# RWKV-7 layer inside a two-layer trunk: output projection tiles moved into the last head pair's products, its queries computed in quarters

## The reference

```python
def wkv7_scan(S0, r, w, k, v, a, b):
    def step(S, inp):
        r_t, w_t, k_t, v_t, a_t, b_t = inp
        sa = jnp.einsum('bhvk,bhk->bhv', S, a_t)
        S = S * w_t[:, :, None, :] + sa[..., None] * b_t[:, :, None, :] + v_t[..., None] * k_t[:, :, None, :]
        return S, jnp.einsum('bhvk,bhk->bhv', S, r_t)
...
    r = heads(xr @ w_rkv[0])
    k = heads(xk @ w_rkv[1])
    v = heads(xv @ w_rkv[2])
...
        y = (y + bonus).reshape(B, L, D_MODEL).astype(dtype)
        return (y * g) @ w_out
```

## Time and profile before

| | us |
|---|---|
| median of 3 runs | 2353.7 (2351.63 to 2355.56) |
| the profiled execution | 2355.08 |
| its span, first to last instruction | 2353.2 |
| TensorE busy | 2275.5 |
| VectorE busy | 1569.6 |
| ScalarE busy | 1267.3 |
| the last pair, from its scores (L1422) to its variance (L1607) | 1261.6 to 1318.0 |

### The profile page before, as it was taken

How to read it: one execution, slowest core, us unless ns; L and a number is a source line. 1 busy time by engine, 2 the same in 40 slices (tenths; PEclk the granted TensorE clock), 3 DMA queues, 4 the chain that set the end, 5 groups by cost and what they waited for, 6 DMA issues and landing times.

```text
span 2353.2 us, 57929 instructions
## 1 busy us (share of the span) xinstructions
PE 2275.5 (97%) x25142; PEld 1872.2 (80%) x25142; DVE 1569.6 (67%) x1784; ACT 1267.3 (54%) x1399; POOL 201.4 (9%) x200
## 2 busy tenths in 40 slices
PE   8999999999999899999998899999999999999998
PEld 4677666888888478888887688888888888888886
DVE  2544685322233676666665288888888888888888
ACT  4422024322232555555554277878787778787774
POOL 2000561100000040000001020000000000000010
PEclk9999999999999999999999999999999999999999
DMA  8556216233232521211102489999999999999994
GB/s 279 196 215 232 91 45 207 72 107 89 90 105 92 166 68 56 62 59 59 56 25 70 182 326 366 375 370 371 386 357 377 364 382 361 378 368 380 360 391 170
DMA packets 228493, 512.00 MB, mean 218 GB/s; under 512 B 15271, under 2 KB 108223, under 8 KB 228031
## 3 DMA queue, kind: packets, MB, share of 16 engines
q1 hardware_dynamic: 225470, 498.61, 58.5%
q10 hardware_dynamic: 1730, 7.10, 0.9%
q0 software_dynamic: 1152, 4.19, 0.6%
HBM read 492.58 MB, written 17.30 MB: 217 GB/s over the span
## 4 chain that ended last, share of the span: by engine, by line
PE 89%; DVE 4%; ACT 3%; DMA 2%; issue 1%; POOL 0%; ACTq 0%; SPq 0%; DVEq 0%
PE bank L1719 27%; PE bank L1749 13%; PE bank L1202 4%; PE bank L1203 3%; PE bank L1204 3%; PE bank L1108 2%; PE bank L1079 2%; PE bank L1080 2%; PE bank L1081 2%; PE bank L1327 2%; PE bank L1363 2%; PE bank L1220 2%; PE bank L1219 2%; PE bank L1221 2%; PE bank L1374 2%
## 5 line engine op out<-in xcount | busy, mean ns | idle before, releaser
L3121 DVE TENSOR_TENSOR w_low<-expert_w,w_high 128x1792 fp32r<-128x1792 f32 (+2 forms) x384 | 771.8, 2024 | 120.8 <-ACT w_high L2283 118.1
L2283 ACT CAST w_high<-expert_w 128x1792 fp32r<-128x1792 f32 (+2 forms) x384 | 652.0, 1701 | 217.0 <-PE bank L1719 144.5
L1719 PE MATMUL bank<-w_high,xg_high 128*128 128x448 f32 x1024 | 294.2, 368 | 4.0 <-DVE xg_low L3111 4.0
L1719 PE MATMUL bank<-w_high,xg_low 128*128 128x448 f32 x1024 | 293.1, 367 | 0.0
L1719 PE MATMUL bank<-w_low,xg_high 128*128 128x448 f32 x1024 | 293.1, 367 | 0.0
L1719 PEld LDWEIGHTS bank<-w_high,xg_high 128*128 128x128 f32 x1024 | 191.6, 189 | 21.3 <-DVE xg_low L3111 4.1
L1719 PEld LDWEIGHTS bank<-w_high,xg_low 128*128 128x128 f32 x1024 | 192.8, 188 | 16.9
L1719 PEld LDWEIGHTS bank<-w_low,xg_high 128*128 128x128 f32 x1024 | 192.9, 188 | 15.8
L1749 PE MATMUL bank<-w_high,hid_high 128*128 128x512 f32 x448 | 175.8, 392 | 0.0
L1749 PE MATMUL bank<-w_high,hid_low 128*128 128x512 f32 x448 | 174.9, 390 | 0.0
L1749 PE MATMUL bank<-w_low,hid_high 128*128 128x512 f32 x448 | 174.7, 390 | 0.0
(11 more groups left out here) (442 smaller groups left out, 4063.8 us busy)
## 6 DMA issues: line engine op xcount, KB each, us to landing
expert_w<-in_moe_w_dram SPq DMA_DIRECT2D x128, 1792.0 KB, 9.7
expert_w<-in_moe_w_dram SPq DMA_DIRECT2D x32, 2048.0 KB, 10.6
arena<-in_mod_w_dram SPq DMA_DIRECT2D x48, 1024.0 KB, 8.3
expert_w<-in_moe_w_dram SPq DMA_DIRECT2D x32, 1536.0 KB, 10.3
arena<-in_ffn_w_dram SPq DMA_DIRECT2D x44, 512.0 KB, 5.1
slot_rows<-arena SPq DMA_DIRECT2D x25, 512.0 KB, 5.5
arena<-in_hy_w_in_dram SPq DMA_DIRECT2D x12, 1024.0 KB, 5.3
arena<-in_rw_w_rkv_dram SPq DMA_DIRECT2D x48, 256.0 KB, 2.9
```

Of the source, the lines that this page charges most:

```text
L1719: last = pe.matmul(bank[b0 + v][:, 0:EH], x[:, k, :], w_[:, kk, v * EH:v * EH + EH], start=(k == 0 and x is XGH and w_ is wh), stop=(k == ...
L2283: act.copy(high_piece(kind, n), piece(kind, ering[q % ERN], n // 2, n % 2))\
L3121: dve.tensor_tensor(piece(kind, low[s], n // 2, n % 2), piece(kind, ering[s], n // 2, n % 2), high_piece(kind, n).bitcast(F32), ALU.subtract)\
```

## The change

Three things are edited. `OUT_LIST` gives the projection tiles a new order: first the 16 tiles of k = 0 to 3 whose sums lie in banks 2 and 3, then the 16 of the same k in banks 6 and 7, then the rest as before. Fourteen tiles are issued inside m, n and the out products of the last pair, two at a time at seven places, and so fourteen fewer after the variance. And the queries of the last pair (`ahead_queries(7, ...)`, issued at the end of pair 6) are computed in four slices of 64 columns where there were two of 128; this makes 16 more products of the source, which are 64 instructions more ahead of the last pair's level loop.

```diff
         OUT_ORDER = (0, 2, 4, 6, 1, 3, 5, 7)
+        OUT_LIST = [(k, m) for ms in (OUT_ORDER[0:2] + OUT_ORDER[4:6], OUT_ORDER[2:4] + OUT_ORDER[6:8]) for k in range(4) for m in ms]
+        OUT_LIST += [(k, m) for k in range(4, KT - 1) for m in OUT_ORDER]
...
+                width = C if j == KT - 1 else P
                 for k in tiles:
-                    for t in range(SEQ // P):
-                        cs = slice(t * P, t * P + P)
+                    for t in range(SEQ // width):
+                        cs = slice(t * width, t * width + width)
...
-                for t in range(first, last):
-                    k, m = t // KT, OUT_ORDER[t % KT]
-                    if t % KT == 0:
+                for k, m in OUT_LIST[first:last]:
+                    if m == 0:
                         pe.wait_ge(sem("ld_out"), 16 * (k + 1))
...
                     d, b = divmod(x, NB)
+                    if x == NB and not more:
+                        out_products(0, 2)
...
+                    if not more and x % 2 == 0:
+                        out_products(2 + x, 4 + x)
...
                 for d in range(2):
+                    if not more:
+                        out_products(10 + 2 * d, 12 + 2 * d)
...
-                    out_products(0, 2)
+                    out_products(14, 16)
...
-                        out_products(2 * st, 2 * st + 2)
+                        out_products(14 + 2 * st, 16 + 2 * st)
...
-                    out_products(16, 19)
+                    out_products(30, 33)
...
-                    out_products(19, 23)
+                    out_products(33, 37)
...
-                    out_products(23, OUT_TILES)
+                    out_products(37, OUT_TILES)
```

## The result

The changed kernel takes 2358.5 us (median of 20 runs), the one before 2353.1: a ratio of 1.0028, 95% interval 1.0020 to 1.0035. It is slower by 0.28%. The profiled execution has a span of 2357.8 us against 2353.2; the changed kernel's profile is 2.6 us ahead where the last pair's queries begin (1252.88 against 1255.49), in code that is the same in both, so the last pair loses more than the two spans differ by. The time lies in the predicted range, but a clear loss had been given 2 chances in 10.

The account below looks back on a forecast made before the run. TensorE, busy nearly all of the span, was taken as the bound, with stops awaiting blocks of its program. Queries 3.6, first round 1.7, switching 1.8 and stops -5.0 gave +2.1 us: median 2355.8, range over the cases 2350.5 to 2359.5.

Parts of the forecast that it names:

- Queries: Last pair's query products: 64 of 64 columns, each costing what one of 128 does, +3.6 us (bounds 0 and +3.6).
- Ahead of the loop: Before the last pair's level loop: a block boundary falls just ahead of it; no cost was put in the sum.
- First round: Level loop's first round: two inner boundaries stop TensorE, the second for 2.0 us; +1.7 us taken, between 0 and +3.7.
- Behind the loop: L1402, after the level loop: its 0.43 us stop goes, since the boundary moves inside the loop and the block is there.
- m, n and out: Last pair's m, n and out products: moved tiles cover the 2.95 and 1.66 us stops; seven insertions cost +1.8 us.
- the tail: Projection tiles after the variance: fourteen fewer take off 6.05 us, and the same 6.05 us come in m, n and out.
- switching: Seven insertions of tiles among 64x64 products, 0.26 us each for changing tile shapes: +1.8 us, bounds 0 and 7 x 0.35.
- A rule against the trace: Skill's rule that block crossings are mostly hidden: moved tiles cover nothing, so the sum would be 3.6 + 1.8 = +5.4 us.
- The rival of a block missed behind the loads: A boundary in wu (L1507) gets its block one weight transfer later: price +2.9, total +5.0 us, 2358.7; chance 0.17.

Follow-up runs that it names:

- e2: Kernel before with the last pair's queries in quarters of 64 columns, no tile moved; 2357.7 us, 5.5 us over before.
- e4: Kernel before with sixteen of the last pair's score products issued twice (64 instructions more ahead of the level loop), nothing else; ratio 1.0001 to before.
- e3: Changed kernel with queries back in halves of 128 columns, tiles still moved, and sixteen score products issued twice; ratio 1.0008 to the kernel before.
- e9: Kernel before with 24 score products issued twice, 96 instructions more ahead of the level loop; ran once, no ratio.
- e7: Kernel before with 32 score products issued twice, 128 instructions more ahead of the level loop; median 2354.8 us, 2.7 us over before.
- e5: Kernel before with projection weights from k = 3 on loaded only after the last pair's g products; -0.13% to +0.06% against before.
- e8: Kernel before with 12 score products issued twice, 48 instructions more ahead of the level loop; -0.19% to +0.04% against before.

## Why the prediction was wrong, step by step

**Queries: +3.6 predicted, +3.57 measured** (queries up to the first score). The distance doesn't go with the columns: 32 rows of 64 columns take 3.6 us, 0.11 us each, as those of 128 do, and those of eight 0.10. That the weight load ahead of each sets it is the reading; no run varied the load.

**Ahead of the loop: nothing predicted, +0.64 measured.** I had placed a boundary "just ahead of the loop" and not asked whether its block is in time. The same 0.6 stands in e2, and in e4 beside the 0.5 us of the added products.

**First round: +1.7 predicted, +2.5 measured.** The two stops stand where they were forecast, 2.31 and 1.78 us, together 2.1 us more than the 1.98 of before, where 2.0 was forecast. Mis-sized by 0.8 us is the rest. The prediction let the clock give 0.3 of the 2.0 back, and it didn't: the second round's L1366 took 1.97 us again, with a granted clock of 0.59 in the changed kernel's 1270 to 1282 us. And outside the stops the round is 0.4 us longer, 0.28 of it idle time ahead of the second round. The whole lies between the 0 and 3.7 us that the prediction named.

**Behind the loop: -0.43 predicted, +1.70 measured. This is the step that failed**: "the boundary ahead of it falls inside the loop, and the block is there when the loop ends". It fell inside, 8 instructions ahead of the jump back, and its block wasn't brought in the 10 us in which the loop went round: the packet came 2.5 us or more after the end. e2, e3 and e4 show the same without the one or the other edit (the block behind the loop comes only when it is over, stops of 0.4 to 1.5 us in L1402 or L1505), e9 and e7 show that it needn't be so with the boundary farther from the jump. But the late request is only one half of the cost. In e3 no weight transfer was running when the loop ended at 1280.38 us, and the packet came in the microsecond from 1281 us, early in the next transfer:

```profile
q1 hardware_dynamic: 65, 0.27, 77.4%
q8 instruction: 1, 0.02, 5.8%
```

e3 has no stop in L1402. In the changed kernel a transfer filled 1286 to 1288 us and the packet came behind it. No run has the shift and the weights held back, so how much of the +1.70 would be left without the transfers is not shown.

**m, n and out: with the tail, -2.8 predicted (1.8 of switching, 4.61 of stops), -2.61 measured.** The size was right and the reason half wrong. In the changed kernel the shift had taken 3.3 us of those stops already (e2: 6.15 us), and by the profiles the tiles cost more there than they bring: 82.12 us with them, 80.80 without. The medians don't show it (ratios 1.0028 and 1.0025). A sum in the prediction is off too, without harm: among the groups 256 instructions take 6.0 us, not 4.3 (72 of them, 32 rows of L1528 and 4 of L1413, take 1.69, 1298.46 to 1300.15), longer than a fetch by either. The two edits cure the same stops, and I had credited one of them with all of it and never laid the shifted grid over the products with the tiles left out.

The sum was +2.1, the last pair's is +5.8, and the median moved by 5.3. Of the difference of 3.7 us the stop ahead of the loop makes 0.6, the first round 0.8, the failed step 2.1, and m, n, out and tail 0.2. The +5.4 us of "A rule against the trace" meets the median's 5.3 by luck: it has none of the stops, and they are there, some worse and some better than before.

The rival of a block missed behind the loads gave 2358.7, next to the 2358.5 that came, and that is in part luck: 1.6 of the 3.7 us arose ahead of the loop, in its first round and in the products from m on. But what it described did happen, twice and smaller: with the block behind the loop, above, and where it said, in L1507. Its condition was met there: TensorE went on in L1405 at 1290.57, the DMA queues are empty from 1290.6 to 1291.3 us, and then the next transfer begins, 0.7 us behind the boundary. From 1292 to 1293 us of the changed kernel the weights run and no block comes:

```profile
q1 hardware_dynamic: 85, 0.31, 79.3%
```

From 1293 to 1294 us, 2.4 us or more behind the restart in L1405 (1290.57), it comes:

```profile
q8 instruction: 1, 0.02, 5.8%
q1 hardware_dynamic: 8, 0.00, 1.4%
```

The stop in L1507 is 1.30 us, where the same place of e2 and e4 has 0.47 and 0.74: 0.6 to 0.8 us of the 2.9 that the rival had priced. That is part of the failed step's 1.70. In e3 the same place has 1.49 us, so in four kernels whose boundaries lie alike there the stop varies from 0.47 to 1.49.

A rule once more against the rows: the changed kernel stops 2.25, 2.31, 1.78, 0.69 and 1.30 us for blocks, and the kernel before 1.98, 0.43, 2.95 and 1.66. The Trainium skill, Runtime: NRT & Kernel Launch, section Instruction fetch mechanics, calls the crossing of a block boundary mostly hidden; the trace disagrees in these stops, where the blocks are used up in less than 3.7 us. The same section says that a jump back out of a window of two pages forces a fetch of the target. Here the trace disagrees too: the loop's 520 instructions lie over three or four blocks, and in the changed kernel rounds 2 to 4 take 9.6 us with no idle time over 0.32 us and, from 1277 us on, no packet of the instruction queue.

## What to carry to other kernels

Where TensorE works through small products, lay the grid of 256 instructions over its program, before and after the change, and give each block 3.7 us: an edit that adds a handful of instructions moves every boundary behind it, and whether one falls inside a loop, or just ahead of a semaphore wait, can be worth more than the edit. Measure two cures for the same stops apart, since they don't add: from m to the end of the tail the tiles brought 2.6 us alone and cost 0.7 to 1.3 beside the shift, by one profile each. Put the cover in one piece between the boundaries that need it, and ask before holding a transfer back which of its readers comes first.

## What the runs showed of the hardware that I had not expected

- A block didn't come while TensorE waited at a semaphore a few instructions behind the boundary. With 34 instructions between them the packet came 1.0 us after the wait's end with the DMA queues empty (e5); with 82 or 98 it came ahead of it (e8, e4).
- With a boundary 8 instructions ahead of a loop's jump back, the next block came in four kernels only after the last round; with 40 or 72 it came in a later round than the first (4.5 and 6.3 us after the boundary was first passed). By what rule the request goes out isn't settled by these runs.
- A running 512 KB weight transfer holds such a block back: 2.5 us after m's start before the change, 1.0 in e5, and the stop 1.2 us shorter; 2.5 us or more after the loop's end in the changed kernel, 0.6 to 1.6 in e3. In the changed kernel and in e8 the packet came in the microsecond in which the transfer ended.
- Blocks that are resident cost nothing: the level loop's rounds 2 to 4 over three or four blocks, in every kernel here, have no idle time over 0.4 us.
